# GpSimd in place of VectorE for the second and third weight sums of a gate and up group

## The reference, cut to what matters

```python
def _swiglu(x, w_gate, w_up, w_down):
    return (jax.nn.silu(x @ w_gate) * (x @ w_up)) @ w_down

x = x + 0.5 * _swiglu(_rmsnorm(x, ffn1_norm[l]), ffn1_w_gate[l], ffn1_w_up[l], ffn1_w_down[l])
...  # attention, x = x + concat(a_out, b_out) @ w_out
x = x + 0.5 * _swiglu(_rmsnorm(x, ffn2_norm[l]), ffn2_w_gate[l], ffn2_w_up[l], ffn2_w_down[l])
x = _rmsnorm(x, final_norm[l])
```

## Time and profile before

| | |
|---|---|
| median of three runs | 1805.3 us (1805.28 to 1805.44) |
| the profiled execution | 1805.36 us, its span 1803.5 us |
| granted TensorE clock | 0.997 of full speed |
| TensorE busy | 1789.8 us (99%) |
| VectorE busy | 1433.9 us (80%) |
| ScalarE busy | 994.1 us (55%) |
| GpSimd busy | 94.0 us (5%) |
| chain of work that ended last | TensorE 91%, VectorE 4%, transfers 2% |

### The profile page before, as it was taken

One profiled execution on the slowest core, in us unless ns is written; L12 is line 12 of the kernel. 1 busy time (PEld: TensorE's weight loads), 2 busy tenths in 40 slices (PEclk: granted clock), 3 DMA queues, 4 the chain that ended last, 5 costly groups with the idle time before them and its releaser, 6 DMA issues.

```text
span 1803.5 us, 21462 instructions
## 1 busy us (share of the span) xinstructions
PE 1789.8 (99%) x8236; PEld 1487.5 (82%) x8236; DVE 1433.9 (80%) x1719; ACT 994.1 (55%) x1232; POOL 94.0 (5%) x79
## 2 busy tenths in 40 slices
PE   9999999999999999999999999999999999999998
PEld 7888888888888888888888888888888887888887
DVE  7889978899988877666666567889978887668875
ACT  7555455555555636565656455555455555345554
POOL 0100000110000000100000000000000110000000
PEclk9999999999999999999999999999999999999999
DMA  9888658886588857645465466788657887578863
GB/s 323 246 253 246 221 195 227 258 248 215 190 261 242 267 174 245 211 164 176 151 201 160 152 230 224 227 259 241 222 196 226 261 247 234 202 229 249 258 201 114
DMA packets 251093, 398.74 MB, mean 221 GB/s; under 512 B 18160, under 2 KB 96752, under 8 KB 250992
## 3 DMA queue, kind: packets, MB, share of 16 engines
q1 hardware_dynamic: 233760, 364.44, 59.8%
q0 software_dynamic: 16320, 31.46, 10.9%
q10 hardware_dynamic: 912, 1.48, 0.2%
HBM read 378.31 MB, written 2.10 MB: 211 GB/s over the span
## 4 chain that ended last, share of the span: by engine, by line
PE 91%; DVE 4%; DMA 2%; SPq 1%; ACT 1%; issue 0%; ACTq 0%; DVEq 0%; POOL 0%
PE psum L2046 55%; PE psum L2100 18%; PE psum L1959 7%; PE psum L2061 6%; PE psum L1964 4%; DVE w_split L1361 1%; DMA w_raw<-in_ffn_down 1%; SPq L567 1%; DVE w_split L1211 0%; ACT w_split L861 0%; DMA w_raw<-in_ffn_up 0%; DMA w_raw<-in_ffn_gate 0%; ACT w_split L745 0%; DVE squares L1522 0%; PE psum L2255 0%
## 5 line engine op out<-in xcount | busy, mean ns | idle before, releaser
L861 ACT ACTIVATE w_split<-w_raw 128x1024 fp32r<-128x1024 f32 (+2 forms) x560 | 550.8, 1001 | 474.0 <-PE psum L2046 288.9
L1361 DVE TENSOR_TENSOR w_split<-w_raw,w_split 128x1024 fp32r<-128x1024 f32 (+2 forms) x560 | 622.9, 1149 | 106.4 <-ACT w_split L861 101.3
L2046 PE MATMUL psum<-w_split,x_split 128*128 128x512 f32 x2832 | 656.1, 390 | 0.5 <-DVE w_split L1361 0.2
L2046 PEld LDWEIGHTS psum<-w_split,x_split 128*128 128x128 f32 x2832 | 529.1, 188 | 114.6 <-DVE w_split L1361 4.0
L2046 PE MATMUL psum<-w_split,h_planes 128*128 128x512 f32 x1920 | 442.2, 390 | 2.3 <-DVE w_split L1211 2.1
L2046 PEld LDWEIGHTS psum<-w_split,h_planes 128*128 128x128 f32 x1920 | 361.1, 188 | 78.7 <-DVE w_split L1211 3.0
L1211 DVE TENSOR_TENSOR w_split<-w_raw,w_split 128x1024 fp32r<-128x1024 f32 (+1 forms) x244 | 283.9, 1190 | 95.8 <-ACT w_split L745 94.2
L745 ACT ACTIVATE w_split<-w_raw 128x1024 fp32r<-128x1024 f32 (+1 forms) x244 | 246.5, 1032 | 205.1 <-PE psum L2046 147.8
L2100 PE MATMUL psum<-w_split,pair_sums 128*128 128x512 f32 x624 | 162.6, 389 | 0.0
L2100 PE MATMUL psum<-w_split,x_split 128*128 128x512 f32 x540 | 142.1, 389 | 0.0
L2100 PEld LDWEIGHTS psum<-w_split,pair_sums 128*128 128x128 f32 x624 | 117.1, 188 | 24.3
(11 more groups left out here) (247 smaller groups left out, 1212.1 us busy)
## 6 DMA issues: line engine op xcount, KB each, us to landing
w_raw<-in_ffn_down SPq DMA_DIRECT2D x64, 1024.0 KB, 6.0
w_raw<-in_ffn_up SPq DMA_DIRECT2D x47, 1024.0 KB, 5.5
w_raw<-in_ffn_gate SPq DMA_DIRECT2D x46, 1024.0 KB, 7.4
w_raw<-in_ffn_gate SPq DMA_DIRECT2D x82, 512.0 KB, 4.5
w_raw<-in_ffn_up SPq DMA_DIRECT2D x80, 512.0 KB, 5.6
w_raw<-in_ffn_up POOLq DMA_DIRECT2D x60, 512.0 KB, 6.2
w_raw<-in_w_in SPq DMA_DIRECT2D x48, 512.0 KB, 4.6
w_raw<-in_w_in SPq DMA_DIRECT2D x24, 1024.0 KB, 5.2
```

The source lines that it names most:

```text
L861: nc.scalar.activation(w_split[:, split_at(c), 0, part[0]:part[1]], w[:, part[0]:part[1]], ACT.Copy).then_inc(hi_made, 1)
L1361: nc.vector.tensor_tensor(w_split[:, split_at(c), 1, part], w[:, part], w_split[:, split_at(c), 0, part].bitcast(F32), ALU.subtract).then_ ...
L2046: ins = mm(psum[:, bank + t, :], x[:, a, t * P:(t + 1) * P], w[:, b, k, :], start=kk == from_ and (a, b) == (0, 0) and t in begins, stop=k ...
```

## The change

The second and third sums of each pair in a group leave VectorE's list and go to GpSimd's, which waits for its own accumulating transfer and then makes them. GpSimd's order in a group becomes: transfer of pair 0, transfer of pair 1, the two sums of pair 0, transfer of pair 2, the two sums of pair 1, the two sums of pair 2. ScalarE's high part of a "sums" job waits for a new semaphore, `group_sums`. The groups of the down projection (`seven_wide`) keep their sums on VectorE.

```diff
-GROUP_SUMS_AT = (2, 5, 5)
...
+                blocks_at = {m: raw_at(ph, i, raw).rearrange("p (q n) -> p q n", n=2 * STRIP) for raw, m in GROUP_PAIR_OF.items()}
+
+                def double_sum(raw, m):
                     k = GROUP_PAIRS[m]
-                    blocks = raw_at(ph, i, raw).rearrange("p (q n) -> p q n", n=2 * STRIP)
                     pool.wait_ge(lo_made, lo_value(seven_base(ph, i) + GROUP_JOBS.index(("blocks", raw))))
-                    nc.gpsimd.dma_start(blocks[:, 0:4:2, :], source(i, 4 + k // 4)[:, k % 4:k % 4 + 2, :],
+                    nc.gpsimd.dma_start(blocks_at[m][:, 0:4:2, :], source(i, 4 + k // 4)[:, k % 4:k % 4 + 2, :],
                                         accum_op=ALU.add).then_inc(block_sums[m], 16)
+
+                def other_sums(m):
+                    b, done = blocks_at[m], 6 * group_count(ph, i) + 2 * m
+                    pool.wait_ge(block_sums[m], 16 * (group_count(ph, i) + 1))
+                    nc.gpsimd.tensor_tensor(b[:, 3, :], b[:, 0, :], b[:, 3, :], ALU.add).then_inc(group_sums, 1)
+                    pool.wait_ge(group_sums, done + 1)
+                    nc.gpsimd.tensor_tensor(b[:, 1, :], b[:, 3, :], b[:, 1, :], ALU.add).then_inc(group_sums, 1)
+
+                double_sum(2, 0)
+                double_sum(4, 1)
+                other_sums(0)
+                double_sum(5, 2)
+                other_sums(1)
+                other_sums(2)
...
                 if kind == "sums":
                     m = pair_of(ph, raw)
-                    act.wait_ge(weight_sums, weight_sums_value(ph, i, m) + sum_steps(ph, m))
+                    if in_group(ph):
+                        act.wait_ge(group_sums, 6 * group_count(ph, i) + 2 * m + 2)
+                    else:
+                        act.wait_ge(weight_sums, weight_sums_value(ph, i, m) + sum_steps(ph, m))
...
                     seven_low(ph, i, n + 2, ph["next_kn"] if at_end and n >= 9 else ph["kn"])
-                    for m in range(3):
-                        if n == GROUP_SUMS_AT[m]:
-                            sum_blocks(ph, i, m)
```

More of the change, by code:

```diff
@@ L99, in hybrid_layer @@
     wide_sums_steps = sum(2 if m in WIDE_SUMMED_BY_TRANSFERS else 3 for m in range(2))
-    group_sums_steps = sum(2 if m in SUMMED_BY_TRANSFERS else 3 for m in range(3))
+    group_sums_steps = 0
     places = [0, 1, 2, 3]
@@ L324, in hybrid_layer @@
         block_sums = [sem(f"block_sums{n}") for n in range(3)]
+        group_sums = sem("group_sums")
         wide_block_sums = [sem(f"wide_block_sums{n}") for n in range(2)]
@@ L434, in hybrid_layer @@
         sum_steps = lambda ph, m: 2 if by_transfer(ph, m) else 3
-        sums_before = lambda ph, k, m: (GROUP_SUMS_AT[k], k) < (GROUP_SUMS_AT[m], m) if in_group(ph) else k < m
         weight_sums_value = lambda ph, i, m: (ph["sums"] + (i - ph["plain"]) * (group_sums_steps if in_group(ph) else wide_sums_steps) +
-                                              sum(sum_steps(ph, k) for k in ((0, 1, 2) if in_group(ph) else (0, 1)) if sums_before(ph, k, m)))
+                                              sum(sum_steps(ph, k) for k in range(m)))
         def raw_at(ph, i, raw):
@@ L677, in add_blocks @@
                 source = weights_of(ph)
-                for raw, m in GROUP_PAIR_OF.items():
-                    if m not in SUMMED_BY_TRANSFERS:
-                        continue
+                blocks_at = {m: raw_at(ph, i, raw).rearrange("p (q n) -> p q n", n=2 * STRIP) for raw, m in GROUP_PAIR_OF.items()}
+                def double_sum(raw, m):
                     k = GROUP_PAIRS[m]
-                    blocks = raw_at(ph, i, raw).rearrange("p (q n) -> p q n", n=2 * STRIP)
                     pool.wait_ge(lo_made, lo_value(seven_base(ph, i) + GROUP_JOBS.index(("blocks", raw))))
-                    nc.gpsimd.dma_start(blocks[:, 0:4:2, :], source(i, 4 + k // 4)[:, k % 4:k % 4 + 2, :],
+                    nc.gpsimd.dma_start(blocks_at[m][:, 0:4:2, :], source(i, 4 + k // 4)[:, k % 4:k % 4 + 2, :],
                                         accum_op=ALU.add).then_inc(block_sums[m], 16)
+                def other_sums(m):
[10 more added lines that the diff above has]
+                other_sums(2)
             def add_wide_blocks(ph, w):
```

## The result

| | before | after |
|---|---|---|
| median of the runs | 1805.3 us | 1836.8 us (1834.44 to 1837.27, 3 runs) |
| ratio | | 1.017, 95% interval 1.0156 to 1.0183 |
| the profiled execution, its span | 1805.36 us, 1803.5 us | 1837.27 us, 1835.5 us |

The account below looks back on a forecast made before the run. TensorE bounds the kernel, busy 1789.8 of 1803.5 us. Per group 0.8 us if GpSimd is always let in, 1.1 with passing over, plus 0.16 fixed: 1.25; twenty groups 25 us, 1805.4+25, say 1830 us; range 1804 to 1852.

Parts of the forecast that it names:

- the walk: One gate and up group followed instruction by instruction in time; with its added terms, a loss of 1.25 us a group.
- No gain: In the groups, sparing VectorE 83 us can win TensorE back only about 1 us, 0.06%.
- An addition's length: GpSimd's 128x512 addition in a group, scaled from its 128x768 multiplication: 1.21 us, or 1.25 with a fixed 0.14 us start.
- VectorE is held up as well: In VectorE's full stretch of a group, VectorE waits about 1.07 us for each GpSimd addition reading SBUF.
- The second half of raw 4, 0.6 us late: In each group, VectorE's low part ends at 1205.72 where TensorE wants it at 1205.14.
- Passed over one time in five: At VectorE's instruction ends, GpSimd misses its turn in one of five meetings, adding 0.2x(2.2-0.8) us a group.
- second rival: In the groups, GpSimd is passed over as a rule: 2.2 us a group, 44 us, 1849 us; chance 0.24.
- Plain 7, 0.2 us late: At the plain chunk behind raw 5, the low part ends at 1210.0, TensorE wants it at 1209.8.
- first rival: In the groups, GpSimd reads without holding VectorE up; 0.7 us of cover hides everything: 1805 us; chance 0.24.
- The third transfer: On GpSimd's queue, issued behind pair 0's two additions, at 1194.2 and not 1193.34, landing at 1200.4.

Follow-up runs that it names:

- those with seven and eight fills: Changed kernel with seven or eight GpSimd fills (128x464, reading nothing) replacing each pair's two additions, ScalarE waiting for the last: 1815.76 us and 1837.58 us.
- the run of additions that nobody waits for: Changed kernel with GpSimd's six additions a group reading constants, 464 columns, into an idle tile, ScalarE waiting for the transfer alone: 1818.81 us, ratio 1.0075.

## Why the prediction was right, and where its steps were off

**The number.** 1830 us was forecast and 1836.8 measured: slower, inside the forecast's own 1817 to 1843. The groups' gaps come to 1.35 us a group where the walk had 1.25. That the totals are so near is in part luck. The walk's 25 us were to lie at raw 4 and plain 7, and at raw 5 where an addition is passed over. Raw 4 and plain 7 lost 12.6+1.7=14.3; 2.0 more lie at raw 5 in one group, and 10.7 at blocks 5, mixed 3 and plain 6, for which it had nothing. The direction, the hold-up of VectorE and the loss at raw 4 aren't luck: the walk gave them and the traces show them.

**No gain.** Right, and shown: without the sums the time stays (ratio 1.0000).

**An addition's length.** 1.21 us with a fixed part that made it 1.25; undisturbed it takes 1.29. Right within some 3%. The estimate from the Trainium skill, "GPSIMD Engine Reference", section 3.1, was 1.12 us; the trace has 1.29, and the measurement decides.

**VectorE is held up as well.** This was the choice that carried the forecast, since no row of before could show it: 1.07 us an addition. Measured: up to 1.10 in the stretch shown, 0.94 in the mean. In eight low parts it is more, 1.5 to 1.65 us: there GpSimd's addition is recorded as begun while its own transfer is still being issued, just behind the start of the low part or just ahead of it, and VectorE waits that time too. VectorE and GpSimd in one of these:

```profile
159.88 2.87 DVE L1376 TENSOR_TENSOR w_split<-w_raw,w_split 128x1024 fp32r<-128x1024 f32 x1
...
159.13 1.20 POOL L682 DMA_DIRECT2D w_raw<-in_ffn_up  x1 [2.84 <-DVE w_split L1376]
159.91 1.75 POOL L688 TENSOR_TENSOR w_raw<-w_raw 128x512 f32<-128x512 f32 x1
```

The Trainium skill, "SBUF — State Buffer", section "Who interferes with whom", calls the pair of ports that the two share an exclusive lock, and has no contention with a GpSimd instruction that only writes. The traces agree with both, on VectorE's side too: 1351 ns beside additions, 1149 beside fills.

**The second half of raw 4, 0.6 us late, 12 us in all.** Measured 0.2 to 1.0 us in 19 groups, 12.6 us in all. Right in place and size. How much of it the hold-up alone makes stays open: with narrower additions for which nobody waits it is 3.5 us, and no run has additions of the full width without the waits.

**Passed over one time in five, 0.28 us a group.** Wrong: it came to nothing. An addition that was passed over beside low parts would wait one of them out whole and take at least 1.22+1.29=2.5 us; the longest of the 120 took 2.39, and in the long stretch each came in at the next end of a VectorE instruction. Five meetings of 4-element powers were too few and too unlike to take a rate from. The second rival (1849 us) falls with this term.

**Plain 7, 0.2 us late.** Only in four groups, 1.7 us in all and not 4. By the walk the low part is done 5.5 us behind pair 2's sums (1204.50 to 1210.0). In the group of 1414.72 it takes 5.2 us, 1436.70 to 1440.70+1.22=1441.92, and TensorE, held at raw 4, wants it no sooner:

```profile
1440.70 1.22 DVE L1376 TENSOR_TENSOR w_split<-w_raw,w_split 128x1024 fp32r<-128x1024 f32 x1
```

**What the walk didn't have.** It walked one group, in the middle of a phase. The three groups ahead of a down projection have VectorE work of another kind between pair 0's transfer and blocks 5 (5.0 us there). And in six groups plain 6 is late (5.7 us); in five of them ScalarE waits for the chunk to land. In one of these, ScalarE, SyncE's transfer of that chunk and TensorE:

```profile
1211.88 3.90 ACT L876 ACTIVATE w_split<-w_raw 128x1024 fp32r<-128x1024 f32 x4 [2.26 <-DMA w_raw<-in_ffn_up]
...
1203.91 0.37 SPq L541 DMA_DIRECT2D w_raw<-in_ffn_up  x1
...
1214.26 2.11 PE L2058 MATMUL psum<-w_split,x_split 128*128 128x512 f32 x8 [1.23 <-DVE w_split L1376]
```

The chunk lands 8.0 us after its issue. In the same five groups the first two accumulating transfers are issued closer together (5.3 us apart and not 6.0): measured from TensorE's plain 6, the first is issued some 0.65 us later than before and the second is not; the longest of the 60 took 9.3 us to land where the longest before took 8.3. That the transfers crowd each other is argued from these times: other groups with the same spacing have no gap, and no run isolates it. The runs don't tie it to one of the two causes either: those with seven and eight fills have the gap (4.8 and 4.0 us), and so has the run of additions that nobody waits for (2.1 us, with the same closer spacing in five of its six groups), against 0.9 us before.

**The weight of the two causes.** This is the step that was wrong. The prediction let the hold-up of VectorE carry the forecast, and by its first rival the time would stay at 1805 us if VectorE weren't held up. Each cause was measured without the other: VectorE's hold-up 14 us (with narrower additions), late sums 32 us, and the change, which has both, 31.5. They don't add up: where VectorE is held up, TensorE is late at raw 4 already, and the late raw 5 then comes in time (in the group shown above, TensorE runs from 1437.84 through raw 5 without another wait); without the hold-up, raw 5 itself is late, 0.5 to 1.5 us. My own theory behind the result had lateness at 8 to 16 us, and fell with the run of eight fills.

**The first rival, 0.7 us of cover.** Its condition was that GpSimd reads without holding VectorE up; that doesn't hold. Its arithmetic was close: nothing lost as long as pair 2's additions take under 3.2 us. The runs put the end of the cover between 2.7 and 3.8 us. And its own counter-argument, that the stretch by VectorE takes them past 3.2 us, is what happened: 3.6 us in the group shown (1433.11 to 1436.70), 3.5 to 4.4 in all. The third transfer, forecast 0.86 us later, is issued 0.2 to 0.5 us later in eleven groups and 0.9 to 1.6 later in the other nine, counted from the issue of the group's first.

**What stays open.** Of the 32.0 us of span, 27 are placed; the rest is too small or too scattered for me to put a cause to. Of those placed, the 5.7 us at plain 6 have no shown cause, nor has the split of the 12.6 us at raw 4 between the hold-up and the late sums.

## What to carry to other kernels

An idle engine isn't free to take work if it must take turns with a busy one, as GpSimd did here with VectorE: cost both sides, the time that the busy engine loses and the time at which the moved work is done, stretched by every instruction that it must wait for. Find how long that result may take before its consumer waits; here two sums could take 2.7 us at no loss and not 3.8, two undisturbed additions needed 2.6, and beside VectorE they took 3.5 to 4.4. Two stalls on one path hide each other, so measure each cause alone before dividing a loss among them.

## What the runs showed of the hardware that I had not expected

Where both had work, GpSimd's additions and VectorE's low parts alternated: at each end the one that waited came in, and none of the 120 additions took the 2.5 us that being passed over would. A 0.29 us addition of VectorE took 2.03 in this way. GpSimd's fills didn't hold VectorE up: with 480 of them its low parts kept their mean of 1149 ns. And beside low parts a GpSimd addition of half the columns took 1.15 and 1.52 us in the mean by line, not half of 1.75 and 2.11: undisturbed it takes 0.73, and what is added, 0.4 and 0.8 us, is near the 0.5 and 0.8 us added to the full additions' 1.29, a wait for a VectorE instruction and not a share of the data.
